# Prompt attention of a hybrid decoder: the projection steps of the next head pair move from turns one to three of each group of four to turns two to four

## The reference, cut to what matters

```python
q = (_rmsnorm(cq, q_norm_g) @ w_qb).reshape(bsz, s, MLA_HEADS, MLA_NOPE + MLA_ROPE)
q_pe = _rope(q[..., MLA_NOPE:], pos)
...
s = jnp.where(mask, s * MLA_SCALE, NEG_INF)      # causal
p = jax.nn.softmax(s, axis=-1).astype(ckv.dtype)
o = jnp.einsum('bshl,lhv->bshv', o_lat, w_uv)
```

## Time and profile before

| what | value |
|---|---|
| median of 3 runs | 3202.15 us (3199.1 to 3204.58) |
| the profiled execution, its own time | 3205.19 us |
| span of the profiled execution | 3203.5 us |
| TensorE busy | 3000.2 us, 94% of the span |
| VectorE busy | 1744.6 us, 54% |
| ScalarE busy | 943.1 us, 29% |
| mean granted TensorE clock | 0.96 |
| prompt attention, first layer, three pairs with steps (365.11 to 509.80 us) | 144.69 us |
| the same, second layer (1937.50 to 2082.20 us) | 144.70 us |

### The profile page before, as it was taken

The page is one execution under the profiler, slowest core; times in us unless marked ns, Lnnn a source line. Parts: engine busy times, 40 slices in busy tenths (PEclk is TensorE's granted clock), DMA queues, the critical chain, the costliest instruction groups (busy, mean ns, idle before and its releaser), DMA issues. The chain is left out here.

```text
span 3203.5 us, 51156 instructions
## 1 busy us (share of the span) xinstructions
PE 3000.2 (94%) x21190; PEld 2656.4 (83%) x21190; DVE 1744.6 (54%) x2823; ACT 943.1 (29%) x1554; POOL 246.8 (8%) x282
## 2 busy tenths in 40 slices
PE   6988898998999999999979889989899999999998
PEld 5975465668999999999979655666599999999998
DVE  4847566553454545544567656655535455445454
ACT  4124454552311111111231335545423111111113
POOL 3000002530000000000030000034200000000000
PEclk8987899998999999999989869999999999999999
DMA  4121102762111111111031220047421212111211
GB/s 105 40 45 39 38 5 79 250 203 69 34 53 41 46 54 46 55 40 40 23 49 41 42 60 11 25 154 230 145 61 34 60 41 60 41 41 40 60 30 70
DMA packets 226583, 207.96 MB, mean 65 GB/s; under 512 B 50260, under 2 KB 195796, under 8 KB 226148
## 3 DMA queue, kind: packets, MB, share of 16 engines
q1 hardware_dynamic: 200744, 119.38, 13.7%
q0 software_dynamic: 25600, 85.11, 8.6%
HBM read 193.58 MB, written 11.05 MB: 64 GB/s over the span
## 5 line engine op out<-in xcount | busy, mean ns | idle before, releaser
L189 PE MATMUL ps<-streamH,upH 128*128 128x344 f32 x2112 | 449.0, 321 | 6.5 <-issue 5.2
L189 PE MATMUL ps<-streamH,upL 128*128 128x344 f32 x2112 | 447.3, 320 | 0.0
L189 PE MATMUL ps<-streamL,upH 128*128 128x344 f32 x2112 | 445.9, 319 | 0.0
L2334 ACT ACTIVATE upH<-hc 128x1024 fp32r<-128x1024 f32 x88 | 93.3, 1061 | 967.8 <-PE ps L189 967.8
L189 PEld LDWEIGHTS ps<-streamH,upH 128*128 128x128 f32 x2112 | 354.5, 188 | 8.8 <-issue 6.6
L189 PEld LDWEIGHTS ps<-streamH,upL 128*128 128x128 f32 x2112 | 356.0, 188 | 0.0
L189 PEld LDWEIGHTS ps<-streamL,upH 128*128 128x128 f32 x2112 | 352.7, 188 | 0.0
L2498 DVE TENSOR_TENSOR xT<-xT,ps 128x1032 f32<-128x1032 f32 x176 | 216.0, 1228 | 227.5 <-PE ps L189 227.5
L458 PE MATMUL ps<-inH,inW 128*128 128x344 f32 (+1 forms) x1248 | 239.6, 328 | 37.7 <-DVE inW L544 37.7
L2459 DVE TENSOR_TENSOR hc<-ps,rstd 128x1032 f32<-128x1032 f32 x44 | 54.2, 1233 | 370.2 <-PE ps L189 370.2
L458 PEld LDWEIGHTS ps<-inH,inW 128*128 128x128 f32 (+1 forms) x1248 | 202.4, 186 | 47.3 <-DVE inW L544 39.2
(11 more groups left out here) (482 smaller groups left out, 4701.1 us busy)
## 6 DMA issues: line engine op xcount, KB each, us to landing
hc<-in_w_ffn_in SPq DMA_DIRECT2D x88, 512.0 KB, 4.0
hc<-in_w_ffn_out SPq DMA_DIRECT2D x44, 512.0 KB, 3.7
big<-in_w_in SPq DMA_DIRECT2D x22, 512.0 KB, 3.9
stream_raw<-in_w_out SPq DMA_DIRECT2D x16, 512.0 KB, 4.0
big<-in_x_prompt SPq DMA_DIRECT2D x2, 2048.0 KB, 10.0
out_y_prompt<-big SPq DMA_DIRECT2D x8, 512.0 KB
scratch_y<-hc SPq DMA_DIRECT2D x16, 136.0 KB, 3.2
scratch_u<-wring SPq DMA_DIRECT2D x4, 516.0 KB, 3.1
```

The costliest lines, as they stand in the source:

```text
L189: last = pe.matmul(self.ps[:, bank + n, 0:NCOL], w, x[:, n * NCOL:(n + 1) * NCOL], start=(k == 0 and i == 0), stop=(k == len(terms) - 1 an ...
L2334: act.activation(upH[u][:, :, :], raw[u], ACT.Copy).then_inc(g_wh[u], 1)
```

## The change

The ten steps of a pair stood in turns 0, 1, 2, 4, 5, 6, 8, 9, 10 and 12 of the 16. Now they stand in turns 1, 2, 3, 5, 6, 7, 9, 10, 11 and 13. Where a step stands in the fourth turn of a group (steps 2, 5 and 8), TensorE issues it ahead of that turn's `scores`; everywhere else it stays behind them. ScalarE's and VectorE's loops are not edited, but their drains follow `step_at`, so they move by a turn as well, and stay behind the exponential and behind the maxima of their turn.

```diff
-        step_at = {v: j for j, v in enumerate((0, 1, 2, 4, 5, 6, 8, 9, 10, 12))}
+        step_at = {v: j for j, v in enumerate((1, 2, 3, 5, 6, 7, 9, 10, 11, 13))}
...
                 for u in range(NU):
                     p, v = u // NV, u % NV
                     transposes(u)
+                    first = v in step_at and v % 4 == 3 and p + 1 < PAIRS
+                    if first:
+                        step(p + 1, step_at[v])
                     if u + 3 < NU:
                         scores(u + 3)
-                    if v in step_at and p + 1 < PAIRS:
+                    if v in step_at and p + 1 < PAIRS and not first:
                         step(p + 1, step_at[v])
                     if v % 4 == 3:
                         values(u // 4)
```

## The result

The changed kernel takes 3233.84 us, the median of 4 runs (3229.07 to 3238.86), against 3203.03 before (4 runs, 3199.1 to 3204.58): ratio 1.0098, 95% interval 1.0078 to 1.0119. It is slower, as forecast (3231, range 3222 to 3243).

A forecast was written before the change was run, and what follows sets the result against it. TensorE's stream was taken as the bound. Per pair +1.77 +2.95 +1.13 -1.25 = 4.6 us, times six 27.6, on 3205.19 gives 3232.8; the runs' median is 3.0 lower, 3229.8; small extras made it 3231, range 3222 to 3243.

The forecast's parts named there:

- The bound: Attention stage: TensorE's stream sets the time and every wait counts in full; busy share 95% in the groups.
- First group: Turns 0 to 3 of a pair: values start at 10.56 us against 8.79 before, +1.77 us a pair.
- the two waits named: First group: TensorE waits 0.7 us for VectorE's drain ahead of step 1, 1.1 for ScalarE's ahead of step 2.
- the little more that the prediction named: Pair one's first group had no wait for the output, so it loses a little more; no size given.
- Second group: Turns 4 to 7 of a pair: values start at 13.3 us against 10.35 before, +2.95 us a pair.
- The fourth wait: Second group: values wait 2.6 us for step 5's drain, queued on VectorE behind maxima that wait for scores.
- Third group: Turns 8 to 11 of a pair: values start at 10.5 us against 9.37 before, +1.13 us a pair.
- Fourth group: Turns 12 to 15 of a pair: turn 13 starts at 1.53 us, step 9 falls inside an existing wait; -1.25 us.
- The clock: Rival, 0.12: the clock falls in the second group's new gaps, 12 to 18 us more, 3243 to 3249.
- the prediction's own signs of being wrong: L1523 does not wait in the second group, or granted clock under 1.00 between 365 and 520 us.
- The faster rival: Rival, 0.05: drains finish in time, only removed waits are left; -2.1 us a pair, -13 in all, 3189.
- The rival that nothing changes: Rival, 0.03: TensorE has unseen slack, so the waits move without cost, 3202 us.

The follow-up runs named there:

- only_group1: Kernel before, with the new turns and order for the first group's steps alone (0, 1, 2): 3209.54 us, ratio 1.0030.
- drain_first: Changed kernel, with VectorE draining the step of a fourth turn (step 5) ahead of that turn's maxima: 3217.07 us, ratio 1.0043 to the kernel before.
- only_group4: Kernel before, with step 9 alone moved from turn 12 to turn 13: 3198.88 us, ratio 0.9990.
- group4_samples: only_group4, with VectorE's small copies for the samples behind the maxima of turn 14 instead of turn 11: 3193.20 us, ratio 0.9977 to the kernel before.
- late_step: Kernel before, with the first step of groups one to three between the next turn's transposes and scores, and step 9 in turn 13: 3193.42 us, ratio 0.9971.
- only_group2: Kernel before, with the new turns and order for the second group's steps alone (3, 4, 5): 3224.05 us, ratio 1.0065.
- gap_filled: Changed kernel, with two spare 512-column products on TensorE behind the scores of each pair's eighth turn: 3230.96 us, ratio 1.0091 to the kernel before.

## Why the prediction was right

The bound: TensorE's stream sets the stage's time, and waits count in full. It held (the groups' busy share, given as 95%, is 96% by its rows). In pair three of the changed kernel the groups last 12.97, 17.35, 13.31 and 10.97 us; the forecast by its steps was 12.99, 15.78, 12.97 and 11.08. That is 0.02 off in the first group, 0.05 in the second where the clock stayed up, 0.34 in the third and 0.11 in the fourth.

First group, forecast +1.77: measured +1.75, by the two waits named (0.59 and 0.90 idle, plus exposed weight loads). only_group1 has the same 12.98. In pair one it is +2.13 (10.90 to 13.03 us), the little more that the prediction named.

Second group, forecast +2.95: measured +2.90 in pair one, where the clock stayed up (12.83 to 15.73). In pair two the group had lasted 13.18 before and not 12.83, with a wait of 0.61 ahead of the values that the prediction, which read pair three alone, didn't see. So there the waits cost 2.55. This and the extra of pair one nearly cancel (each once in a layer). The fourth wait, called 2.6 from start to start, is 2.39 of idle time. drain_first takes it away by letting the drain past the maxima, and nothing else: the group then lasts 13.25 us. The Trainium skill's rule (Perfetto Trace Analysis, section "Tensor Engine Instruction (MATMUL, LD_WEIGHTS)"), that VectorE keeps its order, agrees with this trace: VectorE was idle for 2.87 us, some 1.3 of them with a finished step that it could have drained.

Third group, forecast +1.13: measured +1.47. The term that was too small is ScalarE's drain of step 8: the sum let it begin 0.20 us after the step, but an exponential (L1591) stands ahead of it, which the prediction named as possible. The third group of pair three, from step 8 (L1475) to the values:

```profile
503.45 1.12 PE L1475 MATMUL ps<-big,wring 128*128 128x512 f32 x2
...
504.39 0.69 ACT L1591 ACTIVATE big<-ps,wring 128x512 f32<-128x512 f32 x1 [0.19 <-DVE wring L1690]
...
505.07 1.18 ACT L1580 ACTIVATE big<-ps 64x512 f32<-64x512 f32 x2
...
506.31 0.44 PE L1523 MATMUL ps<-cst,wring 128*128 128x128 f32 x2 [0.66 <-ACT big L1580]
```

Step 8 starts 7.97 us into the group, just as forecast. The drain starts at 505.07 and not at some 504.6, and the values wait for it.

Fourth group, forecast -1.25: measured -1.36. only_group4 alone gave just 0.80, because there the small copies stood in the way, which the reasoning of that run had left out; group4_samples shows it. The prediction had left them out as well: it took 1.53 us for turn 13 from the last pair, which has no such copies. That this term came out is in part luck, since the longer third group happened to move them out of the way.

The clock: a rival with a chance of 0.12, and it came half true. The forecast had no term for it. In four of six pairs it added 1.62 us in the profiled execution, 6.5 us in all; the rival had six falls of 2 to 3 us each. So one of the prediction's own signs of being wrong came true: the granted clock was under 1.00 in this stretch (0.98 over the three pairs, 0.90 in the second group of pair two). The second group of pair three lasted 17.35 us and not 15.8, and the three pairs 162.25 and not 158.5. The waits alone come to 4.76 us in pair three (with 15.73 for its second group), some 28.7 us in all (35.2 less 6.5), against the 27.6 of the working. The measured 30.8, with an interval of 25 to 38 us, holds both 28.7 and 35.2. How much of the forecast's nearness (3231 is 28.9 over the 3202.15 before) is due to the part of the clock that it left out can't be told.

The faster rival is out: the removed waits did give their time (late_step takes the waits away without the new ones, at -8.9 us), but in the changed kernel the drain behind the maxima outweighed them, at the place that was named. The rival that nothing changes is out too.

What stays open is what decides in which pairs the clock falls. The same 2.39 us gap with the same work around it was followed by either level: in the changed kernel in pairs two and three of each layer, in only_group2 in pair one of each. The medians don't say how many falls the other timed runs have: the waits alone would give 28.7 of the 30.8, and drain_first, whose profile loses 14.9 us of waits and 6.5 of clock, is only 16 less, but both differences are uncertain by some us.

## What to carry to other kernels

When work that goes through a shared buffer is moved, follow the consumer's queue as well as the producer's: here step 5, issued ahead of the scores, gained nothing, since the engine that drains it kept the scores' maxima in front. Keep as much other work between two users of a one-deep buffer as the drain takes (here 1.2 us against one transpose of 0.11), and look for the place where a step fits into a wait that exists anyway, as step 9 did. Walk one period from start-to-start distances in the trace; the period repeats, so each tenth of a microsecond counts as often as the loop runs.

## What the runs showed of the hardware

A gap of 2.39 us on TensorE, with some 2.5 us of work and a gap of 0.97 ahead of it, was followed by the lower clock level (1.2 GHz) in six of twelve cases (four in the changed kernel, two in only_group2), and the values behind it took 4.10 instead of 2.48 us. Filled to 0.67, it was followed by it in none of six. But the clock also fell behind a gap of only 1.03 us: in the fourth group of one pair each of gap_filled and only_group4 (12.66 and 13.23 us instead of 10.97 and 11.54, granted clock 0.87). In the other pairs of both the same 1.03 us gap left the clock at 1.00, and so did the gap of 1.57 in every pair of the kernel before. So in these runs the length of a gap alone doesn't tell whether the clock falls.
